# The first two weight slots of each stage worked off together, k-tile by k-tile, in a hybrid decoder step on one core

## The chip, the cores and the metric

One Trainium2 chip, one core. The metric is the device time of one execution in microseconds (us), as the median of several timed runs. TensorE (PE in the profile) does the matmuls, VectorE (DVE), ScalarE (ACT) and GpSimd (POOL) the elementwise work, SyncE (SP) starts nearly all transfers.

## The reference

One inference step of a two-layer decoder, for a prompt of 256 tokens and 8 x 8 tokens of running sequences, 320 tokens in all, model width 1024, float32. Each layer, cut to what matters:

```python
x = x + 0.5 * swiglu(rmsnorm(x, ffn1_norm), ffn1_w_gate, ffn1_w_up, ffn1_w_down)
z = rmsnorm(x, mix_norm) @ w_in                    # 2048 columns for four mixers
att  = moba_attention(q, k_past + k, v_past + v)   # with RMS-normed q and k
pool = pool_mixer(...); conv = conv_module(...); gmlp = spatial_gating(...)
x = x + concat(att, pool, conv, gmlp) @ w_out
x = x + 0.5 * swiglu(rmsnorm(x, ffn2_norm), ffn2_w_gate, ffn2_w_up, ffn2_w_down)
```

where swiglu(x) = (silu(x @ w_gate) * (x @ w_up)) @ w_down, and rmsnorm(x, g) = x * rsqrt(mean(x * x) + eps) * g.

## The kernel before

**Layout.** Everything is held transposed: channels on the 128 partitions, the 320 tokens along the row. x is 8 tiles of 128 x 320, called d or k (0 to 7). A product of float32 precision is made of three matmuls in the faster float32r format: each operand is split into a rounded part and a rest (hi and lo), and a tile of weights gives hi x hi, hi x lo and lo x hi (lines 538, 539, 541).

**Stages.** A layer is six stages in a row: first gate-up (BASE_G1), down (D1), input projection (I), output projection (O), second gate-up (G2), down (D2). Between I and O stand the mixers' small matmuls.

**Slots.** Weights are used in iterations of four slots, (i, j) with j = 0 to 3. In gate-up, I and O a slot is one output tile, 8 k-tiles of 128 x 128 weights, thus 24 matmuls into PSUM bank j. For each slot SP loads `raw` (line 337), ScalarE rounds it to `w_hi` (`round_slot`, line 813), GpSimd makes `w_lo` (line 434) and counts up `split`; TensorE waits for `split`, and at the end of the slot counts up `slots`, which lets ScalarE write the next weights to this place. SP loads the next raw when `w_lo` has been made. So the chain for the next iteration's slot is: TensorE done, w_hi, w_lo, TensorE again.

**Norms.** A stage's input tile k is x times the gain: ScalarE makes `xg_hi` (line 798) and the square of x (line 805), VectorE makes `xg_lo` (line 1011) and adds the square to `sumsq` (line 1019). The factor 1/rms is not applied to the input: it is multiplied into the output as VectorE takes it from PSUM. For it `sum_squares` (line 551) sums over the partitions by a matmul with ones, into bank 6; ScalarE takes the root (line 794), VectorE the reciprocal (line 1023). ScalarE does the root before it rounds slot (1, 0) in program order; in gate-up it loads the silu table between the two. Norm 0 is that of G1, 1 of I, 2 of G2.

**Down and output projection.** As each output tile d is done, `residual` (lines 1053 to 1068) on VectorE does three things in this order: adds it to x(d) (line 1063), makes xg_lo(d), adds the square of d. ScalarE does in turn, for each slot of O, w_hi of the next iteration's slot, then xg_hi(d) and the square (lines 984 to 988). In O a tile d is one slot, in the down stages it is four.

**Order around the change.** Every engine has its own program, written out by hand, and runs it in order; semaphores join them. At a stage's first slot TensorE waits for each input tile k just ahead of its three matmuls (`ready`, line 557; in O for `mix_ok`, line 782, in the order of tiles `MIX_ORDER`, line 310). The sum follows slot 0, for norm 0 slot 1 (line 559). `bank_free` (line 546) waits until VectorE has taken the bank's last content; banks 0 to 3 are used in turn in gate-up, I and O, banks 4 and 5 in down. In stage I SP loads between the weight slots also the pages of the key and value cache (`load_past`, line 352), in one fixed row: (2, 0), pages, (2, 1), pages and so on to (3, 3). ScalarE rounds slot (3, 1) before it takes the root for the q/k norm (line 907).

Of the kernel before, what the change touches and what calls it, by code (L numbers as in the profile page):

```python
# [81 lines left out]
STORED_STEP, HISTORY_STEP = 7, 4  # L82
# [14 lines left out]
def hybrid_decoder(nc, xT, w8, w11, gains, vecs, consts, pool_w, conv_pw, sp_wT, sp_b,  # L97
# [3 lines left out]
    with ctx:  # L101
# [426 lines left out]
        def _(pe):  # L528
            pe.sem_inc(slots.sem, 4)

            def use_slot(L, base, i, j, out, k_tiles, in_hi, in_lo, first, last, before_k=None):

                pe.wait_ge(split.sem, L * split.per + (base + i) * 4 + (j + 1 + split.head))
                for n, k in enumerate(k_tiles):
                    if before_k:
                        before_k(n, k)
# [16 lines left out]
            def column(L, base, tile0, norm, i, j, first=False):  # L553

                bank_free(L, i * 4 + (tile0 + j))

                ready = (lambda n, k: pe.wait_ge(xg_lo_ok.sem, L * xg_lo_ok.per + norm * DT + k + 1)) if first and j == 0 else None
                use_slot(L, base, i, j, bank[j][:, 0:TOK], range(8), xg_hi, xg_lo, True, True, ready)
                if first and j == (1 if norm == 0 else 0):
                    sum_squares(L, norm)  # L560

            def columns(L, base, tile0, norm, i, first=False):
                for j in range(4):
                    column(L, base, tile0, norm, i, j, first)
# [11 lines left out]
            def gate_up(L, base, tile0, norm):  # L576
                columns(L, base, tile0, norm, 0, first=True)
                with pe.Fori(1, IT_G) as i:
                    columns(L, base, tile0, norm, i)
# [165 lines left out]
            for L in range(DEPTH):  # L745
# [32 lines left out]
                with pe.Fori(0, IT_O) as i:  # L778
                    for j in range(4):
                        bank_free(L, i * 4 + (T_O + j))  # L780
                        counts = dict(MIX_ORDER)
# [657 lines left out]
```

## Time and profile before

| | us |
|---|---|
| timed runs: median (lowest, highest) of 3 | 1197.0 (1196.15, 1201.56) |
| the profiled execution: its own time | 1203.46 |
| its span, first to last instruction | 1201.6 |
| TensorE busy | 1171.2 (97%) |
| GpSimd busy | 808.6 (67%) |
| VectorE busy | 634.1 (53%) |
| ScalarE busy | 530.7 (44%) |

The mean granted clock of TensorE is 0.997 of full speed. The chain of work that ended last goes through TensorE for 90% of the span and through VectorE for 8%. In the timeline a row is an instruction or a run of like ones: start, duration, engine, line of the kernel, operation, what it writes and reads, count, and in brackets how long its engine had been idle and what ended that. Matmul rows overlap: each is longer than the step from one to the next.

### The profile page before, as it was taken

How to read it: one execution, taken by the hardware profiler on the slowest of the kernel's cores; microseconds unless marked ns; L12 is line 12 of the kernel's file. 1: busy time of each engine (PE TensorE's matmuls, PEld its weight loads, DVE VectorE, ACT ScalarE, POOL GpSimd, SP SyncE). 2: the span in 40 equal slices, each digit the busy share in tenths (PEclk: the TensorE clock that was granted, in tenths of full speed). 3: DMA queues.
4: the chain of work that ended last, by engine and by line, in shares of the span. 5: the costliest groups of instructions: out<-in, count | busy, mean ns of one | idle time of the engine just before them, and what ended most of it. 6: DMA issues, size and time to landing. Idle time of an engine off the chain costs nothing.

```text
span 1201.6 us, 23236 instructions
## 1 busy us (share of the span) xinstructions
PE 1171.2 (97%) x7924; PEld 1143.8 (95%) x7924; DVE 634.1 (53%) x897; ACT 530.7 (44%) x778; POOL 808.6 (67%) x424
## 2 busy tenths in 40 slices
PE   5999999999999999999999999999998999999999
PEld 4999999999889999999999999999986999999998
DVE  6657773137976544432255777612679664445100
ACT  4544444443655344444444444444446554444332
POOL 4876767766856766667677676677577466666674
PEclk9999999999999999999999999999999999999999
DMA  7544435457235544435555444455672354444453
GB/s 255 163 149 148 152 114 146 151 187 210 85 108 176 158 146 151 144 118 151 158 180 164 149 141 147 122 154 167 187 220 70 110 156 148 151 148 134 134 147 111
DMA packets 70970, 180.57 MB, mean 150 GB/s; under 512 B 9866, under 2 KB 24850, under 8 KB 70930
## 3 DMA queue, kind: packets, MB, share of 16 engines
q1 hardware_dynamic: 70640, 178.97, 47.5%
q10 hardware_dynamic: 290, 1.10, 0.2%
q8 instruction: 22, 0.36, 0.1%
q14 instruction: 18, 0.15, 0.0%
HBM read 176.45 MB, written 3.58 MB: 150 GB/s over the span
## 4 chain that ended last, share of the span: by engine, by line
PE 90%; DVE 8%; DMA 1%; issue 1%; ACT 1%; SPq 0%; DVEq 0%; ACTq 0%
PE bank L538 29%; PE bank L541 29%; PE bank L539 29%; DVE xg_lo L1011 2%; DVE bank L1088 1%; DVE sumsq L1019 1%; DMA x<-in_xT 1%; DVE prob L1222 0%; PE bank L742 0%; PE bank L695 0%; PE bank L586 0%; DVE qk L1182 0%; DVE prob L1196 0%; DVE tmp L1231 0%; PE bank L718 0%
## 5 line engine op out<-in xcount | busy, mean ns | idle before, releaser
L434 POOL TENSOR_TENSOR w_lo<-raw,w_hi 128x1024 fp32r<-128x1024 f32 (+2 forms) x352 | 766.6, 2182 | 374.8 <-ACT w_hi L813 374.8
L813 ACT ACTIVATE w_hi<-raw 128x1024 fp32r<-128x1024 f32 (+2 forms) x352 | 338.4, 962 | 481.3 <-PE bank L541 453.8
L538 PE MATMUL bank<-xg_hi,w_hi 128*128 128x320 f32 x1664 | 521.4, 313 | 18.6 <-DVE xg_lo L1011 18.6
L539 PE MATMUL bank<-xg_lo,w_hi 128*128 128x320 f32 x1664 | 517.2, 311 | 0.0
L541 PE MATMUL bank<-xg_hi,w_lo 128*128 128x320 f32 x1664 | 517.1, 311 | 0.0
L538 PEld LDWEIGHTS bank<-xg_hi,w_hi 128*128 128x128 f32 x1664 | 314.4, 189 | 24.3 <-issue 12.7
L539 PEld LDWEIGHTS bank<-xg_lo,w_hi 128*128 128x128 f32 x1664 | 314.5, 189 | 0.8
L541 PEld LDWEIGHTS bank<-xg_hi,w_lo 128*128 128x128 f32 x1664 | 314.5, 189 | 0.0
L538 PE MATMUL bank<-h_hi,w_hi 128*128 128x320 f32 x704 | 217.9, 309 | 0.0
L539 PE MATMUL bank<-h_lo,w_hi 128*128 128x320 f32 x704 | 217.9, 309 | 0.0
L541 PE MATMUL bank<-h_hi,w_lo 128*128 128x320 f32 x704 | 217.8, 309 | 0.0
L1041 DVE TENSOR_TENSOR h_lo<-tmp,h_hi 128x320 f32 x88 | 173.9, 1976 | 74.2 <-ACT h_hi L821 74.2
L1063 DVE SCALAR_TENSOR_TENSOR x<-bank,x 128x320 f32 x48 | 23.4, 487 | 220.7 <-PE bank L541 220.7
L541 PEld LDWEIGHTS bank<-h_hi,w_lo 128*128 128x128 f32 x704 | 132.2, 188 | 0.0
L538 PEld LDWEIGHTS bank<-h_hi,w_hi 128*128 128x128 f32 x704 | 132.2, 188 | 0.0
L539 PEld LDWEIGHTS bank<-h_lo,w_hi 128*128 128x128 f32 x704 | 132.2, 188 | 0.0
L1036 DVE TENSOR_TENSOR tmp<-bank,rms 128x320 f32<-128x320 f32 x88 | 43.0, 489 | 164.4 <-PE bank L541 164.2
L1011 DVE SCALAR_TENSOR_TENSOR xg_lo<-x,gain,xg_hi (+1 forms) x48 | 70.7, 1484 | 46.0 <-ACT xg_hi L798 39.3
L817 ACT ACTIVATE tmp<-tmp 128x320 f32<-128x320 f32 x88 | 40.7, 462 | 66.2 <-DVE tmp L1034 66.1
L1039 DVE TENSOR_TENSOR tmp<-tmp 128x320 f32<-128x320 f32 x88 | 52.2, 593 | 6.9 <-ACT tmp L817 2.2
L821 ACT ACTIVATE h_hi<-tmp 128x320 f32 (+1 forms) x88 | 41.3, 469 | 20.6 <-DVE tmp L1039 20.6
L1116 DVE SCALAR_TENSOR_TENSOR conv_y<-conv_in,vec,conv_y 128x64 f32<-128x64 f32 x88 | 48.4, 591 | 0.0
(171 smaller groups left out, 717.9 us busy)
## 6 DMA issues: line engine op xcount, KB each, us to landing
raw<-in_w SPq DMA_DIRECT2D x224, 512.0 KB, 3.8
raw<-in_w SPq DMA_DIRECT2D x64, 384.0 KB, 3.1
raw<-in_w SPq DMA_DIRECT2D x64, 320.0 KB, 2.9
k_all<-in_cache_kT SPq DMA_DIRECT2D x32, 128.0 KB, 2.8
v_past<-in_cache_v SPq DMA_DIRECT2D x32, 128.0 KB, 2.8
x<-in_xT SPq DMA_DIRECT2D x2, 640.0 KB, 6.0
cst<-in_consts ACTq DMA_DIRECT2D x1, 997.0 KB
out_yT<-x SPq DMA_DIRECT2D x1, 960.0 KB, 5.0
```

The source lines that it names most:

```text
L434: pool.tensor_tensor(w_lo[:, j, 0:count * P], raw[:, j, 0:count * P], w_hi[:, j, 0:count * P].bitcast(F32), ALU.subtract).then_inc(split.s ...
L538: pe.matmul(out, hi, in_hi[:, k, :], start=first and n == 0, stop=False)
L539: pe.matmul(out, hi, in_lo[:, k, :], start=False, stop=False)
L541: mm = pe.matmul(out, lo, in_hi[:, k, :], start=False, stop=last and end)
L813: act.activation(w_hi[:, j, 0:count * P], raw[:, j, 0:count * P], ACT.Copy).then_inc(split_hi.sem, 1)
L817: act.activation(tmp[:, 2 + m, :], tmp[:, m, :], ACT.Silu).then_inc(silu_ok.sem, 1)
L821: act.activation(h_hi[:, bass.ds(i * 2 + m, 1), :].rearrange("p a t -> p (a t)"), tmp[:, 6 + m, :], ACT.Copy).then_inc(h_hi_ok.sem, 1)
L1011: dve.scalar_tensor_tensor(out=xg_lo[:, bass.ds(d, 1), :].rearrange("p a t -> p (a t)"), in0=one, scalar=gain[:, bass.ds(gain_col, 1)], in ...
L1036: dve.tensor_tensor(tmp[:, 4 + m, :], bank[2 * m + 1][:, 0:TOK], rms[:, :], ALU.mult).then_inc(taken.sem, 1)
L1039: dve.tensor_tensor(tmp[:, 6 + m, :], tmp[:, 2 + m, :], tmp[:, 4 + m, :], ALU.mult).then_inc(h_ok.sem, 1)
L1041: dve.tensor_tensor(h_lo[:, bass.ds(i * 2 + m, 1), :].rearrange("p a t -> p (a t)"), tmp[:, 6 + m, :], h_hi[:, bass.ds(i * 2 + m, 1), :].b ...
L1116: dve.scalar_tensor_tensor(out=y, in0=window, scalar=weight, in1=y, op0=ALU.mult, op1=ALU.add).then_inc(batch_taps.sem, 1)
```

## The change

`use_pair` takes the first two slots of a stage together: it waits for both slots' weights, and for each k-tile, after one wait for this tile, does the three matmuls of slot 0 into bank 0 and the three of slot 1 into bank 1. Both slots are given back at the pair's end. `first_columns` uses it at the start of G1, I and G2. For norms 1 and 2 the sum of squares is issued inside the pair, ahead of its seventh k-tile (`SUM_STEP = 6`); for norm 0 it stands behind slot 2. In O the loop over two iterations is written out, and its first two slots are a pair too, in the order of MIX_ORDER. `bank_free` of the pair is that of bank 1, the later one. The other engines' programs are unchanged.

```diff
+            def use_pair(L, base, i, j, outs, k_tiles, in_hi, in_lo, before_k):
+                pe.wait_ge(split.sem, L * split.per + (base + i) * 4 + (j + 2 + split.head))
+                for n, k in enumerate(k_tiles):
+                    before_k(n, k)
+                    cols, end = slice(n * P, (n + 1) * P), n == len(k_tiles) - 1
+                    for e in range(2):
+                        pe.matmul(outs[e], w_hi[:, j + e, cols], in_hi[:, k, :], start=n == 0, stop=False)
+                        pe.matmul(outs[e], w_hi[:, j + e, cols], in_lo[:, k, :], start=False, stop=False)
+                        mm = pe.matmul(outs[e], w_lo[:, j + e, cols], in_hi[:, k, :], start=False, stop=end)
+                        if end:
+                            mm.then_inc(slots.sem, 1)
...
-                if first and j == (1 if norm == 0 else 0):
+            def first_columns(L, base, tile0, norm):
+                def ready(n, k):
+                    if n == SUM_STEP and norm:
+                        sum_squares(L, norm)
+                    pe.wait_ge(xg_lo_ok.sem, L * xg_lo_ok.per + norm * DT + k + 1)
+                bank_free(L, tile0 + 1)
+                use_pair(L, base, 0, 0, [bank[e][:, 0:TOK] for e in range(2)], range(DT), xg_hi, xg_lo, ready)
+                column(L, base, tile0, 0, 2)
+                if norm == 0:
                     sum_squares(L, norm)
+                column(L, base, tile0, 0, 3)
...
-                with pe.Fori(0, IT_O) as i:
-                    for j in range(4):
-                        bank_free(L, i * 4 + (T_O + j))
-                        counts = dict(MIX_ORDER)
-                        ready = (lambda n, k: pe.wait_ge(mix_ok.sem, mix_ok.at(L, counts[k]))) if j == 0 else None
-                        use_slot(L, BASE_O, i, j, bank[j][:, 0:TOK], [k for k, _ in MIX_ORDER], mix_hi, mix_lo, True, True, ready)
+                counts, order = dict(MIX_ORDER), [k for k, _ in MIX_ORDER]
+                bank_free(L, T_O + 1)
+                use_pair(L, BASE_O, 0, 0, [bank[e][:, 0:TOK] for e in range(2)], order, mix_hi, mix_lo,
+                         lambda n, k: pe.wait_ge(mix_ok.sem, mix_ok.at(L, counts[k])))
+                for i, j in ((0, 2), (0, 3), (1, 0), (1, 1), (1, 2), (1, 3)):
+                    bank_free(L, i * 4 + (T_O + j))
+                    use_slot(L, BASE_O, i, j, bank[j][:, 0:TOK], order, mix_hi, mix_lo, True, True)
```

TensorE's program at the start of the input projection, layer 0, before: the last k-tiles of slot 0 (bank 0), the sum (bank 6), the first matmul of slot 1 (bank 1). Names in brackets are the semaphores waited for.

```order
L538 MATMUL bank0<-xg_hi_55,w_hi_50 128x320 [waits xg_lo_ok]
L539 MATMUL bank0<-xg_lo_56,w_hi_50 128x320
L541 MATMUL bank0<-xg_hi_55,w_lo_51 128x320
L538 MATMUL bank0<-xg_hi_55,w_hi_50 128x320 [waits xg_lo_ok]
L539 MATMUL bank0<-xg_lo_56,w_hi_50 128x320
L541 MATMUL bank0<-xg_hi_55,w_lo_51 128x320
L551 MATMUL bank6<-sumsq_75,ones_60 128x320 [waits summed]
L538 MATMUL bank1<-xg_hi_55,w_hi_50 128x320 [waits split,taken]
```

And the same place now: the sixth k-tile for both banks, the sum, the seventh.

```order
L558 MATMUL bank0<-xg_hi_55,w_hi_50 128x320 [waits xg_lo_ok]
L559 MATMUL bank0<-xg_lo_56,w_hi_50 128x320
L560 MATMUL bank0<-xg_hi_55,w_lo_51 128x320
L558 MATMUL bank1<-xg_hi_55,w_hi_50 128x320
L559 MATMUL bank1<-xg_lo_56,w_hi_50 128x320
L560 MATMUL bank1<-xg_hi_55,w_lo_51 128x320
L549 MATMUL bank6<-sumsq_75,ones_60 128x320 [waits summed]
L558 MATMUL bank0<-xg_hi_55,w_hi_50 128x320 [waits xg_lo_ok]
```

The sum stood behind 24 matmuls of its stage, and stands behind 36 now, ahead of the last two k-tiles of both slots.

For norm 0, the first gate-up, the same in TensorE's program before: the end of slot 1, the sum, the start of slot 2.

```order
L538 MATMUL bank1<-xg_hi_55,w_hi_50 128x320
L539 MATMUL bank1<-xg_lo_56,w_hi_50 128x320
L541 MATMUL bank1<-xg_hi_55,w_lo_51 128x320
L551 MATMUL bank6<-sumsq_75,ones_60 128x320 [waits summed]
L538 MATMUL bank2<-xg_hi_55,w_hi_50 128x320 [waits split,taken]
L539 MATMUL bank2<-xg_lo_56,w_hi_50 128x320
```

And now: the end of slot 2, the sum, the start of slot 3.

```order
L537 MATMUL bank2<-xg_lo_56,w_hi_50 128x320
L539 MATMUL bank2<-xg_hi_55,w_lo_51 128x320
L549 MATMUL bank6<-sumsq_75,ones_60 128x320 [waits summed]
L536 MATMUL bank3<-xg_hi_55,w_hi_50 128x320 [waits split,taken]
L537 MATMUL bank3<-xg_lo_56,w_hi_50 128x320
L539 MATMUL bank3<-xg_hi_55,w_lo_51 128x320
```

The sum moved from behind 48 matmuls to behind 72.

In the output projection, TensorE's first matmuls before:

```order
L533 ISA [waits taken]
L538 MATMUL bank0<-mix_hi_53,w_hi_50 128x320 [waits mix_ok,split]
L539 MATMUL bank0<-mix_lo_54,w_hi_50 128x320
L541 MATMUL bank0<-mix_hi_53,w_lo_51 128x320
L538 MATMUL bank0<-mix_hi_53,w_hi_50 128x320 [waits mix_ok]
```

And now, where bank 0 is finished with the 45th matmul of the stage, bank 1 with the 48th; before, with the 24th and the 48th:

```order
L558 MATMUL bank0<-mix_hi_53,w_hi_50 128x320 [waits mix_ok,split,taken]
L559 MATMUL bank0<-mix_lo_54,w_hi_50 128x320
L560 MATMUL bank0<-mix_hi_53,w_lo_51 128x320
L558 MATMUL bank1<-mix_hi_53,w_hi_50 128x320
L559 MATMUL bank1<-mix_lo_54,w_hi_50 128x320
L560 MATMUL bank1<-mix_hi_53,w_lo_51 128x320
```

Each wait now stands ahead of six matmuls in place of three.

## Rows read from the trace of the kernel before

**Rows 1.** waits of TensorE over the whole span: us in total, times, longest us

```profile
PE bank L538 <- DVE xg_lo L1011: 18.6, 8, 10.1
```

**Rows 2.** timeline, start of input projection, layer 0: start us, us, what, [idle before]

```profile
251.51 0.31 PE L538 MATMUL bank<-xg_hi,w_hi 128*128 128x320 f32 x1
...
254.45 0.31 PE L541 MATMUL bank<-xg_hi,w_lo 128*128 128x320 f32 x1
...
255.93 0.48 DVE L1019 TENSOR_TENSOR sumsq<-sumsq,square 128x320 f32<-128x320 f32 x1
...
256.06 0.41 PE L538 MATMUL bank<-xg_hi,w_hi 128*128 128x320 f32 x1 [1.30 <-DVE xg_lo L1011]
...
256.59 0.70 PE L551 MATMUL bank<-sumsq,ones 128*128 128x320 f32 x2
...
257.76 1.05 ACT L813 ACTIVATE w_hi<-raw 128x1024 fp32r<-128x1024 f32 x1
```

**Rows 3.** timeline, start of layer 0 (same columns)

```profile
14.54 0.47 PE L538 MATMUL bank<-xg_hi,w_hi 128*128 128x320 f32 x1
...
14.80 0.47 PE L539 MATMUL bank<-xg_lo,w_hi 128*128 128x320 f32 x1
...
15.83 5.18 POOL L434 TENSOR_TENSOR w_lo<-raw,w_hi 128x1024 fp32r<-128x1024 f32 x2
...
18.70 2.66 DVE L1019 TENSOR_TENSOR sumsq<-sumsq,tmp 128x320 f32<-128x320 f32 x1
...
25.59 0.81 PE L551 MATMUL bank<-sumsq,ones 128*128 128x320 f32 x2 [1.06 <-DVE sumsq L1019]
```

**Rows 4.** timeline, first gate-up of layer 1: sum matmul and GpSimd's w_lo

```profile
615.52 0.70 PE L551 MATMUL bank<-sumsq,ones 128*128 128x320 f32 x2
...
619.24 15.54 POOL L434 TENSOR_TENSOR w_lo<-raw,w_hi 128x1024 fp32r<-128x1024 f32 x6 [8.19 <-ACT w_hi L813]
```

**Rows 5.** timeline, output projection of layer 0

```profile
343.76 0.40 PE L538 MATMUL bank<-mix_hi,w_hi 128*128 128x320 f32 x1
...
347.20 0.42 PE L538 MATMUL bank<-mix_hi,w_hi 128*128 128x320 f32 x1 [0.56 <-DVE mix_lo L1262]
...
352.68 0.48 DVE L1063 SCALAR_TENSOR_TENSOR x<-bank,x 128x320 f32 x1
...
353.11 2.41 POOL L434 TENSOR_TENSOR w_lo<-raw,w_hi 128x1024 fp32r<-128x1024 f32 x1 [1.11 <-ACT w_hi L813]
...
354.01 1.86 DVE L1011 SCALAR_TENSOR_TENSOR xg_lo<-x,gain,xg_hi  x1 [0.85 <-ACT xg_hi L798]
```

**Rows 6.** timeline, layer 0, start of the second gate-up

```profile
372.83 0.31 PE L538 MATMUL bank<-xg_hi,w_hi 128*128 128x320 f32 x1
...
376.90 0.48 DVE L1019 TENSOR_TENSOR sumsq<-sumsq,square 128x320 f32<-128x320 f32 x1
...
377.03 0.42 PE L538 MATMUL bank<-xg_hi,w_hi 128*128 128x320 f32 x1 [0.96 <-DVE xg_lo L1011]
...
377.57 0.70 PE L551 MATMUL bank<-sumsq,ones 128*128 128x320 f32 x2
```

**Rows 7.** timeline around the q/k norm, layer 0 and (last two) layer 1

```profile
291.94 1.06 ACT L813 ACTIVATE w_hi<-raw 128x1024 fp32r<-128x1024 f32 x1 [4.82 <-DMA raw<-in_w]
...
298.49 0.49 DVE L1079 TENSOR_TENSOR z_w<-bank,rms 128x320 f32<-128x320 f32 x1 [1.08 <-PE bank L541]
...
301.86 0.20 DVE L1189 COPY k_all<-qk 128x64 f32<-128x64 f32 x1
...
302.37 2.38 POOL L434 TENSOR_TENSOR w_lo<-raw,w_hi 128x1024 fp32r<-128x1024 f32 x1 [3.04 <-ACT w_hi L813]
...
302.40 2.40 DVE L1189 COPY k_all<-qk 128x64 f32<-128x64 f32 x1
...
888.32 0.49 DVE L1079 TENSOR_TENSOR z_w<-bank,rms 128x320 f32<-128x320 f32 x1 [2.05 <-PE bank L541]
...
891.80 2.80 DVE L1188 COPY q_pad<-qk 64x64 f32<-64x64 f32 x2
```

More of the change, by code:

```diff
@@ L80 @@
 NC_ = sum(n for _, n in CONSTS)
-STORED_STEP, HISTORY_STEP = 7, 4
+STORED_STEP, HISTORY_STEP, SUM_STEP = 7, 4, 6
 SMALLS = 6
@@ L529, in _, with use_slot @@
             pe.sem_inc(slots.sem, 4)
-            def use_slot(L, base, i, j, out, k_tiles, in_hi, in_lo, first, last, before_k=None):
+            def use_slot(L, base, i, j, out, k_tiles, in_hi, in_lo, first, last):
                 pe.wait_ge(split.sem, L * split.per + (base + i) * 4 + (j + 1 + split.head))
                 for n, k in enumerate(k_tiles):
-                    if before_k:
-                        before_k(n, k)
                     hi, lo = w_hi[:, j, n * P:(n + 1) * P], w_lo[:, j, n * P:(n + 1) * P]
@@ L551, in sum_squares @@
                 pe.matmul(bank[6][:, 0:TOK], ones[:, :], sumsq[:, :], start=True, stop=True).then_inc(norm_sum.sem, 1)
-            def column(L, base, tile0, norm, i, j, first=False):
-                bank_free(L, i * 4 + (tile0 + j))
-                ready = (lambda n, k: pe.wait_ge(xg_lo_ok.sem, L * xg_lo_ok.per + norm * DT + k + 1)) if first and j == 0 else None
-                use_slot(L, base, i, j, bank[j][:, 0:TOK], range(8), xg_hi, xg_lo, True, True, ready)
-                if first and j == (1 if norm == 0 else 0):
+            def use_pair(L, base, i, j, outs, k_tiles, in_hi, in_lo, before_k):
[9 more added lines that the diff above has]
+                            mm.then_inc(slots.sem, 1)
@@ new lines, in column, with columns @@
+            def column(L, base, tile0, i, j):
+                bank_free(L, i * 4 + (tile0 + j))
+                use_slot(L, base, i, j, bank[j][:, 0:TOK], range(8), xg_hi, xg_lo, True, True)
+            def columns(L, base, tile0, i):
+                for j in range(4):
+                    column(L, base, tile0, i, j)
+            def first_columns(L, base, tile0, norm):
[7 more added lines that the diff above has]
+                if norm == 0:
@@ L576, in gate_up @@
             def gate_up(L, base, tile0, norm):
-                columns(L, base, tile0, norm, 0, first=True)
+                first_columns(L, base, tile0, norm)
                 with pe.Fori(1, IT_G) as i:
-                    columns(L, base, tile0, norm, i)
+                    columns(L, base, tile0, i)
             def qk_sums(L):
```

23 lines of the change are left out of this document (10 added, 13 removed).

## The prediction

> **What bounds the kernel now.** Four views were read, in this order. The page first: TensorE is busy for nearly all of the span, so only its pauses can be won, and each stall put into it costs in full. Then the waits of TensorE: the one large entry is that for the last normalised input tile, 18.6 us in 8 waits; 10.1 us of it is the arrival of x at the start [rows 1]. Then the timeline at each of the eight stage starts that the edit touches, and last the timelines of VectorE, GpSimd and ScalarE there, since they make the tiles and weights that TensorE waits for.
>
> The reader is to see one pattern: at a stage start TensorE works off seven k-tiles of slot 0, 21 matmuls 0.147 us apart (251.51 to 254.45), and stands until xg_lo of tile 7 exists, at 256.06 in place of 254.59: 1.47 us, with the slower first matmul 1.56 [rows 2]. Slot 0 and slot 1 together would give it 42 matmuls, 6.2 us, before that tile. The same row pattern stands at the second layer's gate-up and input projection; before the second gate-up's last tile it is 1.0 (377.03), and in the output projection, where the 19th matmul would follow at 343.8 + 18 x 0.147 = 346.48, it comes at 347.20 [rows 5, 6]. If nothing else moved, the change would save 3 x 1.56 + 2 x 1.0 + 2 x 0.8 = 8.3 us. Three things do move: both slots are given back only at the end of the pair, the sum matmul moves, and the pair starts on the later of two slots and banks.
>
> I write slot (i,j) for iteration i, place j. Times are those of the profiled execution of before, shifted where I say so.
>
> **1. Start of layer 0: +1.5 us.** Slot 0 is worked off now as its first tiles come (the matmuls at 14.54 and 14.80 are its). The pair needs w_lo of slot 1, and GpSimd has it when it begins the next one, at 15.83 [rows 3]. So the early work on slot 0 falls away. From 15.9 on, 48 + 24 matmuls precede the sum (it now stands behind slot 2 for this norm; the sums of squares are done by 25.59, so that it waits no longer). At 0.147 each the sum would start at 26.5. But the first burst after a standstill ran at 0.267 (14.54 to 14.80) [rows 3]; 20 such would put it at 28.9. Behind the sum hang root, the load of the silu table, w_hi(1,0) and w_lo(1,0), and these took 619.24 - 615.52 = 3.72 us to GpSimd's start in layer 1, and 15.54/6 = 2.59 for the first part [rows 4]: 6.3 us. The sum itself takes 0.54 (0.70 from start to end, 0.16 of it beside the next matmul [rows 6]). TensorE has after it only 0.54 + 3.53 us of work (slot 3), where before it had 0.54 + 7.05. So slot (1,0) starts 6.3 us after the sum: at 32.8 to 35.2, against 25.59 + 7.6 = 33.2 now [rows 3], -0.4 to +2.0. I take +1.5, near the end that the slow rows give.
>
> **2. First gate-up of layer 1: +0.7 us.** Pair from 615.52 - 7.05 - 1.56 = 606.9, no pause, sum after 72 matmuls at 617.5 (615.52 now). Slot (1,0) would follow at 621.5, but its w_lo is there at 617.5 + 6.3 = 623.8; now it starts at 615.52 + 0.54 + 7.05 = 623.1 [rows 4]. The 1.56 us saved are lost again to a new wait of 2.3 us for GpSimd. Ends: -1.6 if the chain were to hide, +0.7.
>
> **3. Input projection, both layers: -5.0 us together.** The sum before the seventh k-tile comes at 251.51 + 36 x 0.147 = 256.8; the squares are complete at 255.93 + 0.48 = 256.4, so it waits for nothing, and stands 0.2 later than now (256.59) [rows 2]. The pair has its last matmul at 258.9, and TensorE is 1.56 ahead. But slot 0 is free only at 258.8, so w_hi(1,0) comes at 258.9 instead of 257.76 [rows 2], and w_lo(1,0), raw(2,0) and the whole queue of SP behind it (loads of weights and pages in a fixed row) 1.15 later. That queue is waited for: ScalarE stood 4.82 us for raw(3,1) at 291.94, and the root of the q/k norm is behind it [rows 7]. VectorE therefore takes z_w at max(298.49 - 1.56, 298.49 - 1.08 + 1.15) = 298.56 in layer 0, no gain (1.08 is what it waited for TensorE there); in layer 1 it waited 2.05 for TensorE there, so 0.9 of gain is left [rows 7]. From there VectorE sets the pace. It was held up in both layers because a small copy met GpSimd's w_lo(3,3): at 302.40, 2.40 us for what took 0.20 at 301.86, against GpSimd's 302.37; and 2.80 for two copies in layer 1 [rows 7]. That w_lo comes 1.15 later with its load, the copies do not, so both pass ahead of it: 2.2 to 2.4 us each. I take 2.0 in layer 0 (nearly all of it is useful, since TensorE was the next one to be late) and 3.0 in layer 1. Ends: 0.9 in all if other two-input operations meet GpSimd instead, 8 if the waits behind vanish too.
>
> **4. Output projection and the gate-up behind it: +3.4 us a layer, +6.8.** This is the dearest part. TensorE loses the 0.8 us pause: the pair ends at 343.8 + 48 x 0.147 = 350.9, and the gate-up could begin at 343.8 + 192 x 0.147 = 372.0 instead of 372.83 [rows 5, 6]. But VectorE makes here one x, one xg_lo and one sum of squares for each slot, and now gets its first tile 2.3 us later and the second at the same time. What a shared stretch with GpSimd costs stands in the rows: while GpSimd ran w_lo back to back (15.83, 5.18 us for two), an addition to sumsq that takes 0.48 elsewhere [rows 6] took 2.66 [rows 3]; and at 354.01 xg_lo took 1.86, to 0.35 us after the end of GpSimd's 353.11 + 2.41 [rows 5]. One two-input operation gets in at each end of a GpSimd instruction. At present the next GpSimd instruction comes a microsecond later, and sumsq passes. After the change slots (0,0) and (0,1) are released 0.44 apart, so w_lo(1,0) and (1,1) run back to back, 351.8 to 354.3 to 356.9. xg_lo(0) gets through at 354.6, sumsq(0) only at 357.1, and x(1), behind it in VectorE's order, starts at 357.1 (352.68 now). Tile 1 meets no GpSimd work, since w_hi(1,2) stands behind its square on ScalarE: x(2) at 357.1 + 1.33 + 0.5 + 0.4 = 359.3 (1.33 from x to xg_lo by 352.68 and 354.01; 0.5 for an unhindered xg_lo and 0.4 to the next start are estimates from the 0.48 of x and sumsq, of the same size) [rows 5, 6]. Then w_lo(1,2) and (1,3) run back to back again, and so on: two tiles take 7.8 us, where TensorE takes 7.05 for two slots. That gives x(5) at 372.7, x(7) at 380.5 and sumsq(7) complete at 382.7, against 376.90 + 0.48 = 377.4 now [rows 6].
>
> The gate-up's pair waits for bank 1, thus for x(5): start 373.2. It reaches the sum at 378.5 and stands until 382.7; with 0.54 for the sum and 12 matmuls the pair ends at 385.0. Now the sum is at 377.57, and with 0.54 + 24 x 0.147 the same work is done at 381.6 [rows 6]. So +3.4, in which the 0.8 and the 1.0 are already counted. Ends: -1.9 if VectorE caught up fully, +1.1 if only the first pair of slots collides.
>
> In the Trainium skill, the page "SBUF — State Buffer", section "SBUF: two separate sides", says that VectorE and GpSimd share one pair of ports as an exclusive lock: the later one stands for the whole instruction of the other. The 2.66 and the 1.86 agree. Were it a split of bandwidth, both going on at a slower pace, term 4 would be about the -1.9 of its lower end; by the lock it is the +3.4.
>
> **Sum.** 1.5 + 0.7 - 5.0 + 6.8 = +4.0 us on the profiled execution's 1203.46 us (span 1201.6). The three timed runs have their median at 1197.0, 6.5 lower; I carry the difference over: 1201.0 us. What is unrolled in the output projection (no loop, eight slots written out) changes no matmul and is counted at nothing: the eight slots' work hides the instruction fetches; of the old loop's branch no row shows a pause of TensorE.
>
> **The rivals.**
> A. It does what it is said to do: VectorE keeps up in the output projection (term 4 at -1.9 a layer), the rest as above: 1.5 + 0.7 - 5.0 - 3.8 = -6.6, 1190.4 us. For it: alone, a tile needs VectorE only 1.33 + 0.5 + 0.4 = 2.2 us, so it has 1.3 us of slack a slot. Against it: the 2.66 row.
> B. Slower: the new stall of TensorE in front of the second gate-up's sum, 4.2 us in each layer, and 2.3 us in each first gate-up, bring its clock down, and the input projection gives only its sure 0.9. In its first burst the rows show 0.267 us a matmul in place of 0.147 [rows 3]: 12 to 20 of these at each of the two long stalls cost 1.4 to 2.4. 1.5 + 0.7 - 0.9 + 6.8 + 2 x 1.9 = +11.9, 1208.9 us. [...] With the clock unchanged it is +8.1, 1205. The page "TensorE: Matmul & The Clock Gate" of the Trainium skill, section "Why this matters for your kernels", also has it that long pauses between bursts bring TensorE back to half clock; no pause of 4 us inside the kernel is in this trace.
> C. The gains vanish behind the chains and so do the losses: VectorE's collisions in the output projection are only the first (+1.1 a layer) and the copies' gain is half: 1.5 + 0.7 - 2.5 + 2.2 = +1.9, 1199 us.
>
> **How the numbers follow.** A difference of under 0.5%, 6 us, counts as none here. My forecast with C beside it (both within 6 us): 0.45 of chance, 0.30 for the forecast and 0.15 for C; B in its two forms 0.37; A 0.18. The predicted time is the forecast's, 1201. The likeliest case alone would be 1197 to 1205. For 8 in 10 the range reaches to most of A and of B: 1191 to 1210. Faster by over 0.5%: 0.18; within: 0.45; slower: 0.37.
>
> **What would show it.** Term 1: the first matmul at 15.9 and a wait of TensorE for GpSimd's w_lo near 32 to 35. Term 2: a wait for w_lo of about 2 us near 621. Term 3: no pause at 254 to 256, the copies behind the q/k norm at 0.2 each. Term 4: sumsq operations of 2.6 us in the output projection, x(7) some 6 us after where it stands, and a wait of TensorE for sumsq of some 4 us twice. If those sumsq rows are 0.48 long, term 4 is wrong and A is right. If the matmuls behind these waits lie 0.267 apart, B is.

## The result, and the profile after

The change makes the kernel slower. In the runs made together the median is 1217.3 us (1214.2, 1214.6, 1220.0, 1225.0), that of the kernel before 1199.0: ratio 1.0175, 95% interval 1.0151 to 1.0200. The forecast was 1201.0, in a range of 1191 to 1210. The prediction had three runs of before, with a median of 1197.0; the fourth run, 1201.01, moved it to 1199.0. The profiled execution of after took 1214.2 us (span 1212.4, mean granted clock 0.990), that of before 1203.5 (1201.6, 0.997).

Where the 10.8 us between the two profiles lie is told best by stages, from TensorE's timeline: the time from the first matmul of a stage to that of the next. The third column is a second profile of the unchanged kernel, made later.

| us | before | before, again | after | after - before |
|---|---|---|---|---|
| start and G1, layer 0 | 174.07 | 173.99 | 178.00 | +3.92 |
| I and mixers, layer 0 | 92.25 | 89.52 | 89.56 | -2.69 |
| O, layer 0 | 29.07 | 29.07 | 29.63 | +0.56 |
| G2, layer 0 | 156.64 | 156.63 | 161.33 | +4.69 |
| G1, layer 1 | 156.99 | 156.98 | 157.59 | +0.60 |
| I and mixers, layer 1 | 94.13 | 93.75 | 91.58 | -2.55 |
| O, layer 1 | 29.09 | 29.07 | 29.64 | +0.55 |
| G2, layer 1 | 156.65 | 156.64 | 162.32 | +5.67 |

The down stages are 77.4 us each in all (80.4 for the last, with the output). Between the two profiles of before every stage but I repeats to 0.1 us, and I does not: layer 0 differs by 2.7 us. This matters a good deal below.

TensorE's waits of after, some of the largest; they stand in the place of [rows 1]. Columns: us in total, times, longest us.

```profile
PE bank L558 <- POOL w_lo L434: 16.1, 1, 16.1
PE bank L549 <- DVE sumsq L1041: 8.2, 2, 4.1
PE bank L536 <- POOL w_lo L434: 3.8, 2, 1.9
PE bank L616 <- DVE tmp L1199: 2.6, 2, 1.5
PE bank L558 <- DVE x L1085: 2.5, 2, 1.2
```

The wait for xg_lo is gone entirely: the change does what it says. In its place TensorE waits for weights (at the start and 1.9 us in each first gate-up), for the reciprocal of the q/k norm (L616, 2.6 in two), for bank 1 (1.2 twice) and for the sum of squares (4.1 twice).

The output projection and the start of the second gate-up, layer 0, of after, VectorE's timeline; it answers to [rows 5, 6]. Columns: start us, us, what, [idle before].

```profile
352.00 0.49 DVE L1085 SCALAR_TENSOR_TENSOR x<-bank,x 128x320 f32 x1 [3.61 <-PE bank L560]
353.62 2.22 DVE L1033 SCALAR_TENSOR_TENSOR xg_lo<-x,gain,xg_hi  x1 [1.14 <-ACT xg_hi L820]
355.77 2.70 DVE L1041 TENSOR_TENSOR sumsq<-sumsq,square 128x320 f32<-128x320 f32 x1
358.39 0.48 DVE L1085 SCALAR_TENSOR_TENSOR x<-bank,x 128x320 f32 x1
...
360.19 0.49 DVE L1041 TENSOR_TENSOR sumsq<-sumsq,square 128x320 f32<-128x320 f32 x1
...
363.62 2.70 DVE L1041 TENSOR_TENSOR sumsq<-sumsq,square 128x320 f32<-128x320 f32 x1
...
374.09 0.48 DVE L1085 SCALAR_TENSOR_TENSOR x<-bank,x 128x320 f32 x1
...
381.88 0.48 DVE L1085 SCALAR_TENSOR_TENSOR x<-bank,x 128x320 f32 x1
...
383.77 0.49 DVE L1041 TENSOR_TENSOR sumsq<-sumsq,square 128x320 f32<-128x320 f32 x1
```

GpSimd at the same time:

```profile
353.08 5.04 POOL L434 TENSOR_TENSOR w_lo<-raw,w_hi 128x1024 fp32r<-128x1024 f32 x2 [8.78 <-ACT w_hi L835]
360.93 5.03 POOL L434 TENSOR_TENSOR w_lo<-raw,w_hi 128x1024 fp32r<-128x1024 f32 x2 [2.82 <-ACT w_hi L835]
```

This is the picture of term 4. All of it comes 1.2 us later than forecast, since the output projection starts at 344.99 and not at 343.76. GpSimd makes w_lo in runs of two. The sumsq of every other tile takes 2.70 us and ends only at 358.47, when GpSimd has stopped at 353.08 + 5.04 = 358.12. Two tiles take 7.8 us. x(5) is at 374.09 (372.7 + 1.2 = 373.9 forecast), x(7) at 381.88 (380.5 + 1.2 = 381.7).

TensorE there, of after:

```profile
374.62 0.42 PE L558 MATMUL bank<-xg_hi,w_hi 128*128 128x320 f32 x1 [1.22 <-DVE x L1085]
...
384.31 1.44 PE L549 MATMUL bank<-sumsq,ones 128*128 128x320 f32 x2 [4.15 <-DVE sumsq L1041]
...
385.81 0.47 PE L559 MATMUL bank<-xg_lo,w_hi 128*128 128x320 f32 x1
386.08 0.47 PE L560 MATMUL bank<-xg_hi,w_lo 128*128 128x320 f32 x1
```

Behind the stall the matmuls lie 0.267 apart (385.81 to 386.08) and the sum takes 1.44 us in place of 0.70. The stretches of after say it by the granted clock. A row has the stretch, its length, the busy us of TensorE, of its weight loads, of VectorE, ScalarE and GpSimd with the number of instructions, then the granted clock as a share of full speed, and the share and GB/s of the DMA engines. The first three rows are the stretch before the sum, the one behind it and the next. Then come two around the sum in layer 1 (whose stall ends at 979.21), the q/k norm of layer 1, and the stretch behind the wait for w_lo in layer 0.

```profile
380.00:384.00 4.00, 0.17 (x2) 0.00 (x0) 3.05 (x4) 1.50 (x3) 1.60 (x1) 0.99 0.75 202
384.00:387.50 3.50, 3.19 (x10) 2.80 (x11) 1.41 (x2) 2.40 (x3) 0.00 (x0) 0.52 0.57 174
387.50:391.00 3.50, 3.50 (x26) 3.50 (x25) 3.25 (x5) 2.60 (x4) 1.99 (x1) 1.00 0.00 0
...
978.00:981.30 3.30, 2.09 (x6) 1.70 (x7) 1.01 (x3) 2.29 (x5) 0.00 (x0) 0.50 0.88 251
981.30:984.70 3.40, 3.40 (x14) 3.40 (x14) 3.30 (x4) 2.72 (x4) 0.48 (x1) 0.50 0.02 6
...
895.90:902.80 6.90, 6.90 (x20) 5.22 (x19) 5.09 (x16) 2.88 (x4) 3.82 (x2) 0.51 0.75 198
...
36.00:39.20 3.20, 3.20 (x14) 3.20 (x13) 2.51 (x3) 1.74 (x3) 3.20 (x2) 0.50 0.49 164
```

0.50 is the lower of TensorE's two levels, 1.2 GHz.

The start of layer 0, of after, for [rows 3]:

```profile
16.05 0.60 PE L558 MATMUL bank<-xg_hi,w_hi 128*128 128x320 f32 x1 [16.05 <-POOL w_lo L434]
...
29.42 0.70 PE L549 MATMUL bank<-sumsq,ones 128*128 128x320 f32 x2
...
35.55 0.47 PE L536 MATMUL bank<-xg_hi,w_hi 128*128 128x320 f32 x1 [1.91 <-POOL w_lo L434]
```

### The profile page after: what moved, and what is told of

It is laid out like the page before. It is cut to its first block, busy times and chain, and to the rows that moved or that the text cites. A ratio compares the mean times of both kernels' runs of the same rounds, so it can differ in the third digit from the quotient of the medians.

```text
span 1212.4 us, 23198 instructions
## 1 busy us (share of the span) xinstructions
PE 1176.5 (97%) x7924; PEld 1150.1 (95%) x7924; DVE 634.0 (52%) x897; ACT 529.0 (44%) x778; POOL 811.6 (67%) x424
## 4 chain that ended last, share of the span: by engine, by line
PE 47%; POOL 23%; issue 21%; SPq 3%; DVE 2%; ACT 1%; DMA 1%; POOLq 1%; DVEq 0%; ACTq 0%
POOL w_lo L434 23%; PE bank L536 14%; PE bank L539 14%; PE bank L537 14%; DVE sumsq L1041 1%; SPq L359 1%; SPq L356 1%; SPq L361 1%; DMA raw<-in_w 1%; PE bank L558 1%; PE bank L559 1%; PE bank L560 1%; PE bank L616 1%; ACT square L827 0%; DMA x<-in_xT 0%
## 5 line engine op out<-in xcount | busy, mean ns | idle before, releaser
L537 PE MATMUL bank<-xg_lo,w_hi 128*128 128x320 f32 x1568 | 486.8, 310 | 0.0
L539 PE MATMUL bank<-xg_hi,w_lo 128*128 128x320 f32 x1568 | 486.6, 310 | 0.0
L536 PEld LDWEIGHTS bank<-xg_hi,w_hi 128*128 128x128 f32 x1568 | 296.5, 189 | 7.9 <-POOL w_lo L434 4.3
L537 PEld LDWEIGHTS bank<-xg_lo,w_hi 128*128 128x128 f32 x1568 | 296.5, 189 | 0.5
L539 PEld LDWEIGHTS bank<-xg_hi,w_lo 128*128 128x128 f32 x1568 | 296.4, 189 | 0.0
L1033 DVE SCALAR_TENSOR_TENSOR xg_lo<-x,gain,xg_hi (+1 forms) x48 | 59.7, 1255 | 46.2 <-ACT xg_hi L820 46.2
```

The costliest lines, as they stand in the source:

```text
L536: pe.matmul(out, hi, in_hi[:, k, :], start=first and n == 0, stop=False)
L537: pe.matmul(out, hi, in_lo[:, k, :], start=False, stop=False)
L539: mm = pe.matmul(out, lo, in_hi[:, k, :], start=False, stop=last and end)
L1033: dve.scalar_tensor_tensor(out=xg_lo[:, bass.ds(d, 1), :].rearrange("p a t -> p (a t)"), in0=one, scalar=gain[:, bass.ds(gain_col, 1)], in ...
```

## The experiments

Nine kernels, and before itself once more. The columns "O + G2" are those two stages together, layer 0 and layer 1; the first profile of before has 174.07 / 156.99, 92.25 / 94.13 and 185.71 / 185.73. The ratio of after is to the 1199.0 above. The others are to runs of before on the same chip, whose medians were 1197.4, 1197.8 and 1197.9 us in the three sets (a set for experiments 1 to 4, 5 to 8, 9 and 10). The stages are those of the one profiled execution of each kernel.

| | median us | ratio (95%) | G1, 0 / 1 | I, 0 / 1 | O + G2, 0 / 1 |
|---|---|---|---|---|---|
| after | 1217.3 | 1.0175 (1.0151-1.0200) | 178.00 / 157.59 | 89.56 / 91.58 | 190.96 / 191.96 |
| 1 pair in I only | 1199.1 | 1.0020 (0.9993-1.0046) | 174.06 / 156.96 | 93.09 / 92.05 | 185.72 / 185.71 |
| 2 pair in O only | 1213.3 | 1.0135 (1.0117-1.0153) | 173.80 / 156.97 | 89.50 / 92.22 | 193.70 / 193.44 |
| 3 O as before | 1199.0 | 1.0001 (0.9983-1.0019) | 175.76 / 157.59 | 91.35 / 90.74 | 184.48 / 184.49 |
| 4 stall filled | 1210.9 | 1.0126 (1.0105-1.0147) | 176.28 / 157.59 | 91.85 / 91.54 | 189.60 / 189.50 |
| 5 norm tile first | 1208.4 | 1.0079 (1.0055-1.0103) | 176.41 / 157.59 | 91.08 / 90.67 | 188.67 / 188.65 |
| 6 sum behind pair | 1195.3 | 0.9971 (0.9946-0.9995) | 174.02 / 155.42 | 92.82 / 94.11 | 184.49 / 184.48 |
| 7 lagged form | 1191.9 | 0.9927 (0.9901-0.9953) | 173.93 / 155.42 | 89.08 / 90.03 | 184.49 / 184.48 |
| 8 before, again | one run, 1200.2 | | 173.99 / 156.98 | 89.52 / 93.75 | 185.70 / 185.71 |
| 9 lagged, I only | 1195.0 | 0.9969 (0.9945-0.9993) | 174.17 / 156.97 | 88.22 / 88.68 | 185.71 / 185.71 |
| 10 lagged, O too | 1201.2 | 1.0023 (1.0001-1.0044) | 174.01 / 155.42 | 89.00 / 89.52 | 190.78 / 190.67 |

### 1. The pair in the input projection alone

```diff
 # kernel before, and
-                columns(L, BASE_I, T_I, 1, 0, first=True)
+                first_columns(L, BASE_I, T_I, 1)
```

> Only the input projection has the pair (with the sum inside); both gate-ups and the output projection as before. My theory (each stage has its own account, and the loss sits in the output projection and the clock behind it): the input projection keeps the gain it has in the changed kernel, -2.7 and -2.6 us, all else stands as before: -5.2, about 1194 us. Rival (the input projection's gain in the changed kernel is borrowed from the stages ahead of it, which were late, so that its queues had more lead): the pair alone gives under 1.5 us in both layers together, and the time is 1198 to 1199.

Measured: 1199.1 us, no gain; by the interval -0.8 to +5.5 us. My theory fell, and the rival's numbers hold. Its reason does not: counted from the first matmul of the stage, the matmul that waits for the reciprocal of the q/k norm comes at 46.25 and 47.11 us here and at 46.47 and 46.85 in after, so after had borrowed nothing. Unchanged input projections have it at 46.87 in both layers of all three profiles (before, experiments 2 and 8). TensorE arrives 1.5 us ahead, waits, and loses 0.9 of these 1.5 us in layer 0 and all of them in layer 1; behind the wait its clock is down. Rows of this kernel: the wait in layer 0 and in layer 1, then the stretch behind the first.

```profile
297.76 3.27 PE L629 MATMUL bank<-tmp,cst 8*128 8x320 f32 x8 [0.88 <-DVE tmp L1211]
...
889.25 1.04 PE L629 MATMUL bank<-tmp,cst 8*128 8x320 f32 x2 [1.73 <-DVE tmp L1211]
```

```profile
299.00:305.80 6.80, 6.80 (x23) 5.63 (x22) 5.81 (x18) 2.55 (x3) 3.44 (x2) 0.51 0.72 207
```

Over the two stages the granted clock is 0.94 and 0.96 here, 0.98 to 1.00 in the unchanged ones. The copies ran free as forecast (0.20 for the longest), and it paid nothing. They did so in all nine profiles with a changed input projection, where none took over 0.90 us.

### 2. The pair in the output projection alone

```diff
 # kernel before, and
-                with pe.Fori(0, IT_O) as i:
...
+                use_pair(L, BASE_O, 0, 0, [bank[e][:, 0:TOK] for e in range(2)], order, mix_hi, mix_lo, ...)
+                for i, j in ((0, 2), (0, 3), (1, 0), (1, 1), (1, 2), (1, 3)):
```

> Only the output projection has the pair; gate-ups and input projection as before. My theory (the two slots released together make GpSimd run back to back and VectorE late): sumsq rows of 2.6 to 2.7 us in the output projection, x(7) at about 381 in place of 376.9, and the second gate-up, slot by slot, stands some 6 us ahead of its last k-tile; with half clock behind that stall +6 to +9 us a layer, 1211 to 1217 us. Rival (the loss needs the pairs in the gate-ups, whose sum comes earlier in TensorE's row): the output pair alone costs 0 to 2 us a layer, 1199 to 1203.

Measured: +8.0 and +7.7 us in O + G2 of the two layers, 15.9 at the medians. My theory holds: this one edit alone loses most of what the whole change loses. The loop written out costs nothing itself: O takes 28.24 us in both layers, which is 192 matmuls 0.147 apart. Without the pair in G2, TensorE stands for tile after tile, at half clock in the end. The waits of this kernel in layer 0, and the stretch:

```profile
371.75 0.41 PE L538 MATMUL bank<-xg_hi,w_hi 128*128 128x320 f32 x1 [0.41 <-DVE xg_lo L1046]
375.12 0.63 PE L538 MATMUL bank<-xg_hi,w_hi 128*128 128x320 f32 x1 [2.67 <-DVE xg_lo L1046]
379.58 0.63 PE L538 MATMUL bank<-xg_hi,w_hi 128*128 128x320 f32 x1 [3.29 <-DVE xg_lo L1046]
```

```profile
376.50:384.40 7.90, 4.82 (x16) 4.43 (x17) 4.47 (x5) 4.73 (x6) 0.78 (x1) 0.50 0.52 159
```

### 3. The changed kernel, output projection as before

```diff
 # kernel after, and the loop of before in O:
-                use_pair(L, BASE_O, 0, 0, ...)
+                with pe.Fori(0, IT_O) as i:
```

> The changed kernel with the output projection as before (a loop, slot by slot); gate-ups and input projection keep their pairs. My theory: no long sumsq rows, no wait for sumsq and no half clock at the second gate-up, which gains its 1.0 us of pause in each layer; with +3.9 and +0.6 of the first gate-ups and -5.2 of the input projections: -2.7, about 1196 us. Rival (the pair in the second gate-up brings a stall and a slow clock of its own): the second gate-up +2 to +4 us a layer, 1202 to 1206.

Measured: 1199.0, no difference from before, between the two ranges. By its stages it went as my theory has it: O + G2 1.2 us under before in each layer, no wait for sumsq, no slow stretch. The stages other than I add up to -0.2 against before. What is missing at the median is again the input projection's gain, which I had put at -5.2.

### 4. The stall filled with matmuls

```diff
 # kernel after, and
+                    if n == SUM_STEP and norm == 2:
+                        for _ in range(28):
+                            pe.matmul(bank[7][:, 0:TOK], w_hi[:, 0, 0:P], xg_hi[:, 0, :], start=True, stop=True)
                     if n == SUM_STEP and norm:
                         sum_squares(L, norm)
```

> The changed kernel with 28 more matmuls (into bank 7, which nobody reads) ahead of the sum of the second gate-up: they fill the 4.15 us for which TensorE stands there, and change nothing else. My theory (the stall lowers TensorE's clock, and that costs beside the stall): the stall's time stays, the half clock behind it goes: -1.7 us in layer 0 and -3.4 in layer 1 against the changed kernel, and less spread from run to run: 1208 to 1213 us. Rival (the slow stretches come from something else than idle time): the second gate-ups keep their half clock, and the time is that of the changed kernel or above, 1217 to 1219.

Measured: 1210.9 against 1217.3, in the range. G2 is 1.33 us shorter than in after in layer 0 and 2.43 in layer 1 (1.7 and 3.4 said), though it does 28 matmuls more. The clock is the cause; of the 6.4 us between the medians these 3.8 are explained. Rows of this kernel: the filler, the sum, and the stretch behind it, which had 0.52 in after.

```profile
380.55 4.27 PE L580 MATMUL bank<-xg_hi,w_hi 128*128 128x320 f32 x28
384.93 0.81 PE L551 MATMUL bank<-sumsq,ones 128*128 128x320 f32 x2
```

```profile
384.50:388.00 3.50, 3.38 (x22) 2.96 (x21) 2.04 (x2) 3.02 (x4) 0.00 (x0) 1.00 0.65 188
```

With the clock up, O + G2 is 3.9 and 3.8 us over before: term 4 had 3.4.

### 5. Norm tile ahead of the weights on ScalarE

```diff
 # kernel after, and
-                        round_slot(L, base_next, i_next, j, HALVES8)
                         norm_tile(L, T_O, 2, 4 * i + j, j % 2)
+                        round_slot(L, base_next, i_next, j, HALVES8)
```

> The changed kernel with one thing turned round on ScalarE in the output projection: norm tile d (its hi part and its square) first, the next iteration's weight slot behind it, so that GpSimd's w_lo(1,1) comes some 4 us behind w_lo(1,0) instead of right behind it. My theory (VectorE is late because GpSimd's two-input instructions stand back to back and a vector addition waits for a whole one): most sumsq rows fall from 2.7 to 0.5 us, x(7) comes at least 2 us earlier, the wait for sumsq in the second gate-up is under 1.5 us and the half clock behind it is gone: the output projection and second gate-up together 3 to 5 us shorter in each layer, 1207 to 1212 us. Rival (VectorE is late only because it gets its first tile 2.3 us later and two at once, whatever GpSimd does): x(7) as in the changed kernel, 1216 to 1219 us.

Measured: 1208.4, in the range (O + G2 2.3 and 3.3 us shorter, 3 to 5 said), and x(7) at 377.64 instead of 381.88, so that the rival is out. But not by the steps I gave: GpSimd still runs in pairs, and four of the eight sumsq are still long, now those of the odd tiles. Rows of this kernel, VectorE and GpSimd:

```profile
353.75 0.49 DVE L1054 TENSOR_TENSOR sumsq<-sumsq,square 128x320 f32<-128x320 f32 x1
...
357.18 2.69 DVE L1054 TENSOR_TENSOR sumsq<-sumsq,square 128x320 f32<-128x320 f32 x1
...
377.64 0.48 DVE L1098 SCALAR_TENSOR_TENSOR x<-bank,x 128x320 f32 x1
```

```profile
354.50 5.03 POOL L434 TENSOR_TENSOR w_lo<-raw,w_hi 128x1024 fp32r<-128x1024 f32 x2 [12.20 <-ACT w_hi L848]
```

Two tiles still take 7.85 us; the even tile passes before each run, and the row of tiles stands half a period earlier. The wait for sumsq falls to 1.0, and a new one of 1.95 for GpSimd's w_lo of slot (0,1), done at 375.18, comes ahead of the pair, with half clock behind it (0.54 at 376.5 to 379.7).

### 6. The norm-0 sum right behind the pair

```diff
 # kernel of experiment 3, and
                 use_pair(L, base, 0, 0, ...)
+                if norm == 0:
+                    sum_squares(L, norm)
                 column(L, base, tile0, 0, 2)
-                if norm == 0:
-                    sum_squares(L, norm)
                 column(L, base, tile0, 0, 3)
```

> The kernel with the output projection as before and pairs elsewhere, with the norm-0 sum moved from behind slot 2 to right behind the pair. My theory (in the first gate-ups the chain sum, root, silu table, w_hi, w_lo of 6.3 us ends last, and 3.5 us more of TensorE's work behind the sum cover it): the waits of 1.9 us for w_lo of slot (1,0) go in both layers, and in layer 1 the pair's gain of 1.56 us stands: layer 0 2 to 3.5 us and layer 1 about 2.2 us shorter than with the sum behind slot 2, 1193 to 1195 us. Rival (TensorE then waits for something else, since slots 0 and 1 are released together and ScalarE and GpSimd make them one after the other): a wait of 1 to 2 us for w_lo of slot (1,1) takes its place and the time stays at 1197 to 1200.

Measured: 1195.3, just above the range. G1 is 1.74 us shorter in layer 0 and 2.17 in layer 1 than in experiment 3. The waits for w_lo are gone and nothing takes their place; layer 1 keeps the full 1.56 against before. In layer 0 my lower bound of 2 was a little high: the sum now waits 0.97 for the squares.

```profile
25.54 0.81 PE L551 MATMUL bank<-sumsq,ones 128*128 128x320 f32 x2 [0.97 <-DVE sumsq L1053]
```

### 7. A lagged form

```diff
 # kernel of experiment 3; in G2, I, and G1 of layer 1 (e = slot, m = k-tile); G1 of layer 0 as before:
+                plan = ([(0, m) for m in range(7)] + [(1, m) for m in range(4)] +
+                        [(0, 7)] + [(1, m) for m in range(4, 8)])
+                # three matmuls for each; slot e is given back behind its own last k-tile;
+                # norms 1 and 2: sum_squares behind (0, 7); norm 0: behind the plan
```

> Another form of the same idea: slot 0's k-tiles 0 to 6, four of slot 1, then slot 0's last k-tile (and for norms 1 and 2 the sum), then slot 1's other four. 12 matmuls, 1.76 us, cover the late tile, and slot 0 is given back 0.2 us later than before, slot 1 not later. In both second gate-ups, both input projections and the first gate-up of layer 1; the start of layer 0 and the output projection are as before. My theory (the pauses for the last tile can be had for nothing if the slots are not given back later): -1.5, 2 x -1.0 for the gate-ups and up to -1.5 for each input projection: 1191 to 1195 us. Rival (a gain of TensorE in the input projection is lost at the q/k norm, which ScalarE's and SP's rows set): only the gate-ups' -3.5 stays or less, 1194 to 1197.

Measured: 1191.9 us (1190.1 to 1193.0), 0.9927 of before (0.9901 to 0.9953), the fastest of all. The three gate-ups give their 1.2, 1.2 and 1.6 us. The medians of this kernel and of before differ by 5.9, so some 2 us are left for the input projections.

### 8. Before, profiled again

The unchanged kernel.

> The kernel before, unchanged, profiled once more. The input projection with its mixers took 92.25 and 94.13 us in the first profile of before, but 89.5 and 92.23 in the run in which only the output projection was changed, though nothing ahead of it was. My theory (the first profile of before fell on an execution 6 us above its median, and the collisions of VectorE's small copies with GpSimd that my forecast counted as a gain to be had are of that execution): another profile of before shows an input projection at least 1.5 us shorter in one layer, its time near 1197. Rival (92.25 and 94.13 are what this code takes): within 0.7 us of these in both layers.

Measured: I in 89.52 and 93.75. Layer 0 is 2.7 us shorter than in the first profile, so the rival fell there; layer 1 is within 0.4. The same stretch of layer 0 in the first profile of before and in this one:

```profile
302.00:305.30 3.30, 3.30 (x15) 3.30 (x14) 3.24 (x6) 3.12 (x6) 2.85 (x3) 0.50 0.71 224
```

```profile
301.00:304.40 3.40, 3.40 (x26) 3.21 (x24) 3.24 (x13) 1.33 (x2) 0.47 (x2) 1.00 0.62 198
```

The copy of 2.40 us [rows 7] took 0.20 this time:

```profile
302.32 0.20 DVE L1189 COPY k_all<-qk 128x64 f32<-128x64 f32 x1
...
889.40 2.29 DVE L1189 COPY k_all<-qk 128x64 f32<-128x64 f32 x1
```

The second of these rows is from layer 1: there the slow copy is present again, as in experiment 2 (2.35 us). So the collision is not of the first execution alone: it came in four of six unchanged input projections. Its own time, 1200.2, isn't near 1197 as I had said.

### 9. The lagged form in the input projection alone

```diff
 # kernel before, and the plan of experiment 7 at the head of I
```

> Only the input projections have the lagged form (slot 0's tiles 0 to 6, four of slot 1, slot 0's last, slot 1's other four); gate-ups and output projection as before. It is the partner of the run with the pair in the input projection alone, which came out at 1.002 of before, and differs from it only in when slot 0 is given back (0.2 instead of 1.15 us late against before). My theory (what the pair wins at the head of the input projection is lost again at the q/k norm, whose weights come by the slots' release): the spread of the q/k root starts up to 1 us earlier than with the pair, TensorE's wait there is under 0.5 us, and less half clock follows: 1193 to 1196 us. Rival (the q/k norm is not reached by when slot 0 is given back, and the two forms are the same): 1197 to 1199 us, with a wait for the q/k reciprocal of 1.2 to 1.7 us in both layers.

Measured: 1195.0, 0.9969 of before (0.9945 to 0.9993), where the pair had 1.0020. Both input projections are the shortest of all, 88.22 and 88.68, and TensorE's waits name no q/k reciprocal: its matmul comes 45.30 and 45.31 us into the stage, and the 1.5 us are kept. ScalarE's root ahead of it comes at 43.5 and 44.4 us of the stage with the pair, and at 42.0 and 42.2 here. Rows of both layers, of experiment 1 and then of this one (the stages start at 251.50, 842.14, 251.61 and 837.39):

```profile
295.01 0.52 ACT L941 ACTIVATE tmp<-bank,stat 8x320 f32<-8x320 f32 x1
...
886.50 0.52 ACT L941 ACTIVATE tmp<-bank,stat 8x320 f32<-8x320 f32 x1
```

```profile
293.60 0.52 ACT L972 ACTIVATE tmp<-bank,stat 8x320 f32<-8x320 f32 x1
...
879.57 0.52 ACT L972 ACTIVATE tmp<-bank,stat 8x320 f32<-8x320 f32 x1
```

The sum stands behind 36 matmuls in both forms and slot 1 ends with the 48th in both. What differs is that slot 0 and bank 0 are done with the 36th matmul instead of the 45th, and that the lagged form starts without waiting for slot 1 and bank 1. So when slot 0 is finished and given back is what counts here.

### 10. The lagged form in the output projection too

```diff
 # kernel of experiment 7, and the same plan for slots (0,0) and (0,1) of O, in the order of MIX_ORDER
```

> The kernel with the lagged form in the gate-ups and the input projection, and now in the output projection too (start of layer 0 as before). Slot 0 of the output projection is given back 1.0 us later than before, slot 1 some 0.8 earlier, so the two releases lie 1.8 us apart, where the pair has 0.4 and before 3.5. w_lo takes GpSimd 2.4. My theory (back-to-back w_lo make VectorE late): w_lo(1,1) still follows w_lo(1,0) with no gap, one or two sumsq rows of 2.6 us come back, but each round of two slots leaves a little more gap, so that VectorE catches up before sumsq(7), and the second gate-up loses under 1 us: within 1.5 us of the kernel without it, 1190 to 1194 us. Rival (once two w_lo lie back to back they stay so, as with the pair): sumsq(7) about 5 us late, a stall of TensorE and half clock behind it, +4 to +6 us a layer: 1200 to 1204 us.

Measured: 1201.2, 9.3 us over experiment 7; O + G2 +6.3 and +6.2. My theory fell and the rival holds: w_lo runs in pairs right to the end, and sumsq(7) comes 5.1 us late, counted from the start of O. Rows of this kernel, sumsq of tiles 0, 2, 4 and 6:

```profile
350.73 2.70 DVE L1085 TENSOR_TENSOR sumsq<-sumsq,square 128x320 f32<-128x320 f32 x1
...
358.58 2.70 DVE L1085 TENSOR_TENSOR sumsq<-sumsq,square 128x320 f32<-128x320 f32 x1
...
366.43 2.69 DVE L1085 TENSOR_TENSOR sumsq<-sumsq,square 128x320 f32<-128x320 f32 x1
...
374.23 2.67 DVE L1085 TENSOR_TENSOR sumsq<-sumsq,square 128x320 f32<-128x320 f32 x1
```

By the order of the programs the loop closes through ScalarE: w_hi(1,2) stands behind square(1), thus behind x(1) and the long sumsq(0); x(2) follows at once, and so does w_hi(1,3), before w_lo(1,2) is done. That step is read from the rows, not tested.

## Why the prediction was wrong

It was wrong in size, in terms 1, 3 and 4. The waits and collisions of the edit came out as described, but the price of a slow clock behind a wait was left out twice, and the gain in the input projection did not exist.

**Term 1, the start: +1.5 said, +3.92 measured.** The sum is at 29.42, just past my range, since 22 matmuls ran at 0.267; slot (1,0) follows 6.1 us later (6.3 said) at 35.55, 2.3 after the 33.2 of before. The other 1.6 is half clock behind the 1.91 us wait, which the term did not have. That part is chance: experiments 3, 4 and 5 have the same code and the same wait with the clock at full rate behind it, and +1.69, +2.21 and +2.34.

**Term 2: +0.7 said, +0.60 measured**, by the steps given, and experiment 6 shows that the place of the sum is the whole of it.

**Term 4: +6.8 said, +11.5 measured.** Stall and chain are as forecast. What failed is the step that adds "0.54 for the sum and 12 matmuls" at 0.147 us each behind a stall of 4.2 us. I had the clock only in rival B, at 1.4 to 2.4 a stall. Experiment 4 gives its price as 1.33 in layer 0 and 2.43 in layer 1; the remaining 3.9 and 3.8 are the term, undersized by about 0.4 a layer.

**Term 3: -5.0 said, -5.2 between the two profiles, and all the same not a gain of the change.** The agreement is luck. Experiment 1 has the same edit alone and wins nothing. The 92.25 and 94.13 us of the first profile were taken as what the input projection costs. Other executions of unchanged code gave 89.52 and 93.75 (experiment 8), 89.50 and 92.22 (experiment 2). That the copies would run free was right. What was wrong is to take 2.0 and 3.0 off for it and to leave out what the edit brings in their place, the wait at the q/k norm and more half clock behind it. An unchanged input projection took 89.5 us twice with its copies free, and 92.2 to 94.1 four times with a slow one. With the pair the copies were free in all twelve (one of them took 0.90), and the stages took 89.6 to 94.1, on average 91.7; with the lagged form 88.2 to 90.0. The "no gain" at the q/k norm in layer 0 was nearly right (46.25 against 46.87 in unchanged code), the 0.9 of gain in layer 1 did not come (47.11).

At the medians the pair even loses here. This is an estimate: from the distance of each median to that of before, take what the other stages changed in the profiles. What is left for the two input projections:

| kernel | median - before | other stages | left for I |
|---|---|---|---|
| after | +18.3 | +16.0 | +2.3 |
| 1, 3, 6 (pair) | +1.6, +1.6, -2.5 | -0.1, -0.2, -4.1 | +1.7, +1.7, +1.6 |
| 4, 5 (pair) | +13.5, +10.6 | +10.5, +8.8 | +3.0, +1.8 |
| 7, 9, 10 (lagged) | -5.9, -2.9, +3.3 | -4.2, +0.1, +8.4 | -1.7, -3.0, -5.1 |
| 2 (unchanged) | +15.9 | +15.4 | +0.5 |

Each value is uncertain by some 2 to 3 us, as the intervals of the ratios are, but the sign is the same in all six kernels with the pair and the opposite in all three with the lagged form.

**From there the forecast counted one thing twice.** The profiled execution lay 6.5 us over the median of the three runs. I carried this over to get 1201.0, that is, I took the slow execution's excess off, and took 5.0 for repairing its collisions off as well. That much of the excess lay in I is read from the two profiles of before (3.1 us between them there, 0.1 elsewhere), not tested.

**The account.** From 1201.0 to 1217.3 are 16.3 us: 2.0 by the median of before (1199.0, not 1197.0), 2.4 in term 1, -0.1 in term 2, 4.7 in term 4, and 7.3 in term 3, which stood at -5.0 and is left with +2.3; the double count is part of these. Where in the input projection an execution at the median spends these 2.3 no profile shows, since the profiled one was the shortest of the four; two of the others were at 1220.0 and 1225.0, the latter with a mean clock of 0.985 against 0.990. This stays open.

**Rival B** had the right mechanism and the right side, and 8.4 us too little: it stood on the lower base and on 0.9 of gain in term 3, and had the start at +1.5. **Rival A** fell with the first sumsq row of 2.70. In before, pauses of 1.0 and 1.56 at the stage starts are followed by matmuls 0.147 apart; this was no guide to 1.9 or 4.1.

## What to carry to other kernels

Work that covers a late input must not delay giving buffers back: the pair in the input projection won nothing, and a shorter cover with slot 0 released 0.2 us late made the input projection the shortest. Before you count on repairing something slow in a profile, look whether it is there in a second profile of the same code, above all if the profiled execution is slower than the median. A new stall of TensorE can cost a stretch at half clock behind it as well as itself: 1.33 and 2.43 us for the two stalls of 4.1 here.

## What the runs showed of the hardware

**Half clock behind short stalls.** After the stall of 4.15 us in after TensorE ran at 0.52 of full clock for 3.5 us, and around the end of the one of 4.04 at 0.50 for 6.7 us. A wait of 1.9 us for w_lo in the first gate-up stands in after and in experiments 3, 4 and 5, in both layers: the half clock followed once in eight times (35.55 us of after, layer 0). Behind the 1.95 and 1.92 us ahead of the pair in experiment 5 it followed in both layers. The Trainium skill, "TensorE: Matmul & The Clock Gate", section "Why this matters for your kernels", has long pauses between bursts bring TensorE back to half clock. The traces agree for 4.15; from which length on it happens, they don't settle, since stalls of about 2 us went both ways. A stall is not even needed: in the first profile of before the clock was at 0.50 from 302.0 to 305.3 though TensorE had not waited in the 4 us ahead; among its matmuls there were the small ones of the q/k norm, 0.27 apart.

**VectorE and GpSimd.** In every kernel whose output projection had its w_lo in runs of two, a two-input addition of VectorE that met the second w_lo took 2.63 to 2.70 us instead of 0.48, and ended some 0.35 us behind GpSimd's run. Two releases 1.8 us apart in place of 3.5 (experiment 10) were enough to start this, and it did not end until the weights of the stage did.
